# RWKV's chunk inverse: corrections of X and its transpose on 32 of 64 columns

## The chip, the cores and the metric

One of the eight cores of a Trainium2 chip runs the whole program. The metric is the device time of one execution in microseconds. The kernel before took 3782.82 us, the median of 3 runs (3780.62 to 3784.01).

## The reference, cut to what matters

The program computes two transformer-like blocks on 512 tokens of width 1024. The first block has four branches; the change sits in the fourth, RWKV-7, with 16 heads of 64. Its recurrence over the tokens is

```python
def step(state, inp):
    r_t, w_t, k_t, v_t, kk_t, b_t = inp
    sk = jnp.einsum('bhvk,bhk->bhv', state, kk_t)
    state = (state * w_t[:, :, None, :] - sk[..., None] * b_t[:, :, None, :]
             + v_t[..., None] * k_t[:, :, None, :])
    return state, jnp.einsum('bhvk,bhk->bhv', state, r_t)
```

The kernel does this in 8 chunks of 64 tokens. Inside a chunk the dependence of each token on the ones before it is a triangular system, so each chunk and head needs the inverse of a unit triangular 64x64 matrix.

## The kernel before, in words

`rwkv_core_phase` (line 1137 on) is one phase among many. Its first TensorE work stands at about 1237 us of the trace and its last at about 1560 us; projections with 512-column matmuls come before and after. It handles the heads in 8 pairs. A pair's 8 chunks of 2 heads are 16 matrices of 64x64, laid out in one plane of 128 partitions by 512 columns: partitions 0 to 63 hold one matrix of a cell, partitions 64 to 127 another, and the 512 columns are 8 cells of 64 (`cell(h, i)`).

The inverse is built by levels. X and its transpose XT start as the inverse of the 2x2 diagonal blocks (`step_lt`, lines 1591 to 1599). Level n, for n from 1 to 5, joins neighbouring blocks of 2^n columns in three steps:

- Y{n}: TensorE forms Y from LM and X, where LM is the system's matrix under the mask of the level. GpSimd makes LM (line 1503, `level_mask`); ScalarE copies Y out of PSUM (line 1443).
- X{n}: TensorE forms the correction from XT and Y, and VectorE subtracts it from X (line 1575).
- XT{n}: TensorE forms the correction of the transpose from Y and XT, and VectorE subtracts it from XT (line 1575). At level 5 only the transpose is needed: Y5 is a product by `cells` (line 1246), and XT5 as well, subtracted at line 1583.

Each of these steps is 16 fp32 matmuls, one for each 64x64 matrix, each with its own weights (64x64) and 64 moving columns. `blocks64` (line 1254) and `cells` (line 1246) issue them alternating between the two diagonal quarters of the array. The trace shows each fp32 matmul as two records of weight load and two of matmul, so a step is 32 records of each. `products` (line 1239) uses all four quarters of the array in turn.

The order of the work is written out by hand. Time goes in blocks `b` of 16 beats. In block b, pair b is prepared (VectorE lines 1605 to 1614, GpSimd 1503, ScalarE 1484 to 1489); pair b-1 goes through list `A` (X0, then Y, X, XT of levels 1 to 4); pair b-2 goes through list `B` (level 5, the transposes of v, kappa, k and beta by `turn`, the masked products Lk, Ak, Ab with their evictions at line 1589, LkV, NU0, WT); pair b-3 goes through its 8 chunks of state recurrence (PE 1354, 1361, 1371, 1378, 1381; VectorE 1624, 1634); pair b-4 is finished (normalisation, lines 1640 to 1660). Each engine takes its part of each beat strictly in program order, and semaphores tie the engines together. Block 1 has only list A and preparation; blocks 3 to 7 have all of it; from block 9 on list A is empty.

Two orders matter below. At beat 2 and 3 VectorE has, in this order: the subtraction for XT5, a state step (1634), three preparations of pair b (1608, 1609, 1611), the subtraction for X1 and the masked eviction of Lk (1589). And TensorE's `turn` of k at beat 4 (`trkt`, line 1261) writes the PSUM bank that Lk is read from, so it waits for that eviction, with everything behind it.

Of the kernel before, what the change touches and what calls it, by code (L numbers as in the profile page):

```python
# [13 lines left out]
ALU = mybir.AluOpType  # L14
# [6 lines left out]
T = 512  # L21
TT = T // P
# [1114 lines left out]
def rwkv_core_phase(k, r, kk, v, sg, a, norm, hs, w, last=()):  # L1137
# [5 lines left out]
    nc = k.nc  # L1143
# [3 lines left out]
    LT, LM, X, XT, Y = (lambda p, n=n: own(5 * (p % 2) + n) for n in range(5))  # L1147
# [7 lines left out]
    cell = lambda h, i: slice(256 * h + 64 * i, 256 * h + 64 * i + 64)  # L1155
    half = lambda q: slice(64 * q, 64 * q + 64)
    chunk = lambda i, q: slice(P * i + 64 * q, P * i + 64 * q + 64)
    by_head = lambda h, i: slice(P * i + 64 * h, P * i + 64 * h + 64)
    quad = lambda ap: ap.rearrange("p (h i c) -> p h i c", h=2, i=TT)
    eight = lambda ap: ap.rearrange("p (n c) -> p n c", c=64)  # L1160
    two_banks = lambda b: k.ps[:, b:b + 2, 0:256].rearrange("p h (i c) -> p h i c", i=TT)
    mask = lambda ap: ap.unsqueeze(1).unsqueeze(1).broadcast_to([P, 2, TT, 64])
    mask8 = lambda ap: ap.unsqueeze(1).broadcast_to([P, 8, 64])
# [10 lines left out]
    A = ["X0"] + [f"{s}{n}" for n in (1, 2, 3, 4) for s in ("Y", "X", "XT")]  # L1174
# [5 lines left out]
    a_made, a_act, a_dve = k.sem("w_a_made"), k.sem("w_a_act"), k.sem("w_a_dve")  # L1180
# [35 lines left out]
    def users_before(s):  # L1216

        n = B.index(s)
        found = [[t for t in range(n) if b in B_BANKS[t]] for b in B_BANKS[n]]
        return [B[f[-1]] if f else None for f in found]  # L1220
# [5 lines left out]
    with nc.Block() as block:  # L1226
# [7 lines left out]
        def _(pe):  # L1234
# [7 lines left out]
            def cells(l, r, b, r_cell=cell):  # L1242
                for h in range(2):
                    for i in range(TT):
                        for q in range(2):
                            ins = nc.tensor.matmul(k.bank(b)[half(q), cell(h, i)], l[half(q), cell(h, i)], r[half(q), r_cell(h, i)], start=True, stop=True)
                return ins

            def blocks64(l, r, b):
                for h in range(2):  # L1250
                    for i in range(TT):
                        for q in range(2):
                            other = k.const("ident")[half(q), half(q)] if r is None else r[half(q), cell(h, i)]
                            ins = nc.tensor.matmul(k.bank(b)[half(q), cell(h, i)], l[half(q), cell(h, i)], other, start=True, stop=True)  # L1254
                return ins

            def turn(src, b, by):
                for i in range(TT):
                    t = slice(i * P, (i + 1) * P)
                    if by is None:  # L1260
                        ins = nc.tensor.transpose(k.bank(b)[:, t], src[:, t], k.const("ident"))
                    else:
                        ins = nc.tensor.matmul(k.bank(b)[:, t], src[:, t], by, start=True, stop=True)
                return ins

            def step_a(p, s):
                b = A.index(s) % 2
                if s == "X0":
                    pe.wait_ge(lt_out, p + 1)
                    if p >= 1:  # L1270
                        pe.wait_ge(*a_out(p - 1, "XT4"))
                    ins = blocks64(XT(p), None, b)
                elif s[0] == "Y":
                    n = int(s[1:])
                    pe.wait_ge(lm_ok, 4 * p + n)
                    pe.wait_ge(*a_out(p, f"X{n - 1}"))
                    ins = blocks64(LM(p), X(p), b)
                elif s[:2] == "XT":
                    pe.wait_ge(*a_out(p, "Y" + s[2:]))
                    ins = blocks64(Y(p), XT(p), b)  # L1280
                else:
                    pe.wait_ge(*a_out(p, "Y" + s[1:]))
                    if s != "X1":
                        pe.wait_ge(*a_out(p, f"XT{int(s[1]) - 1}"))
                    ins = blocks64(XT(p), Y(p), b)
                ins.then_inc(a_made, 1)

            def step_b(p, s):
                b = B_BANKS[B.index(s)][0]
                for user in users_before(s):  # L1290
                    if user is not None:
                        pe.wait_ge(*b_out(p, user))
                    else:
                        pe.wait_ge(lt_read, min(p + 2, PAIRS))
                        if p >= 1:
                            pe.wait_ge(*b_out(p - 1, "Ab"))
                if s == "Y5":
                    pe.wait_ge(lm5_ok, p + 1)
                    pe.wait_ge(*a_out(p, "X4"))
                    ins = cells(LM(p), X(p), b)  # L1300
                elif s == "XT5":
                    pe.wait_ge(*b_out(p, "Y5"))
                    ins = cells(Y(p), XT(p), b)
                elif s == "trv":
                    ins = turn(pl(v + p), b, None)
                elif s == "trkap":
                    ins = turn(pl(sg + p), b, None)
                elif s == "trkt":
                    pe.wait_ge(pool_ok, 6 * p + 6)
                    ins = turn(pl(kk + p), b, None)  # L1310
                elif s == "trbt":
                    ins = turn(pl(a + p), b, None)
                elif s == "Lk":
                    pe.wait_ge(pool_ok, 6 * p + 6)
                    ins = products(pl(kk + p), pl(sg + p), b)
                elif s == "Ak":
                    ins = products(pl(kk + p), pl(r + p), b)
                elif s == "Ab":
                    ins = products(pl(a + p), pl(r + p), b)
                elif s == "LkV":  # L1320
                    pe.wait_ge(*b_out(p, "Lk"))
                    pe.wait_ge(*b_out(p, "trv"))
                    ins = cells(LKK, VT(p), b, by_head)
                elif s == "NU0":
                    pe.wait_ge(*b_out(p, "LkV"))
                    pe.wait_ge(*b_out(p, "XT5"))
                    ins = cells(XT(p), LKV, b)
                elif s == "WT":
                    pe.wait_ge(*b_out(p, "trkap"))
                    for i in range(TT):  # L1330
                        for q, h in ((0, 0), (1, 1), (0, 1), (1, 0)):
                            ins = nc.tensor.matmul(k.bank(b + q)[half(h), 64 * i:64 * i + 64], KAPT[half(q), by_head(h, i)], XT(p)[half(q), cell(h, i)],
                                                   start=True, stop=True)
                ins.then_inc(b_made, 1)
# [51 lines left out]
            for b in range(BLOCKS):  # L1386
                for beat in range(16):
                    if 3 <= b < PAIRS + 3:
                        p, j = b - 3, beat // 2
# [33 lines left out]
                    for m in range(*gate_steps(b, beat)):  # L1423
                        n, q = divmod(m, KT)
                        if n < len(last):
                            if q == 0:
# [3 lines left out]
                                if n >= 4:  # L1430
                                    pe.wait_ge(gate_out, n - 3)
                            ins = nc.tensor.matmul(k.bank(n % 4), slot(n)[:, q * P:(q + 1) * P], last[n][1](q), start=(q == 0), stop=(q == KT - 1),
                                                   skip_group_check=True)
# [127 lines left out]
        def _(dve):  # L1561
            link = lambda ins: k.dve_chain(dve, ins)

            def step_a(p, s):
                if not on_dve(s):
                    return
                dve.wait_ge(a_made, a_made_at(p, s))
                x = XT(p) if s[1] == "T" else X(p)
                if s == "X1":
                    dve.wait_ge(*a_out(p, "X0"))  # L1570
                elif s == "XT1":
                    dve.wait_ge(lt_out, p + 1)
                else:
                    dve.wait_ge(*a_out(p, s[:-1] + str(int(s[-1]) - 1)))
                nc.vector.tensor_tensor(x, x, k.bank(A.index(s) % 2), ALU.subtract).then_inc(a_dve, 1)

            def step_b(p, s):
                if not on_dve(s):
                    return
                dve.wait_ge(b_made, b_made_at(p, s))  # L1580
                if s == "XT5":
                    dve.wait_ge(*a_out(p, "XT4"))
                    ins = nc.vector.tensor_tensor(XT(p), XT(p), k.bank(2), ALU.subtract)
                elif s == "WT":
                    out = WR(p).rearrange("p (i b c) -> p i b c", i=TT, b=4)[:, :, 0::3, :].rearrange("p i q c -> p q i c")
                    ins = nc.vector.tensor_tensor(out, two_banks(2), before(p).rearrange("p i q -> p q i").unsqueeze(3).broadcast_to([P, 2, TT, 64]), ALU.mult)
                else:
                    dst, m = {"Lk": (LKK, strict), "Ak": (AK(p), incl), "Ab": (AB(p), incl)}[s]
                    ins = nc.vector.tensor_tensor(quad(dst), two_banks(2), mask(m), ALU.mult)
                ins.then_inc(b_dve, 1)  # L1590
# [1475 lines left out]
```

## Time and profile before

| what | value |
|---|---|
| time, median of 3 runs | 3782.82 us |
| the profiled execution's own time | 3787.06 us |
| its span in the trace | 3785.3 us |
| mean granted TensorE clock | 0.951 of full speed |
| PE busy | 3411.5 us (90%) |
| DVE busy | 1218.5 us (32%) |
| ACT busy | 580.8 us (15%) |
| POOL busy | 684.1 us (18%) |

PE is TensorE's matmul side and PEld its weight loads; DVE is VectorE, ACT ScalarE, POOL GpSimd. Busy time is a union: overlapping records count once, and a record's time includes the latency until its result is written. PEclk is the granted TensorE clock as a share of 2.4 GHz; it has two levels, 1.00 (2.4 GHz) and 0.50 (1.2 GHz), and a mean between them says how long each held.

### The profile page before, as it was taken

Reading aid. Unit: us, or ns where it says so; the run is one execution under the profiler, and the core shown is the slowest. Engines: PE = TensorE matmul, PEld = TensorE weight load, DVE = VectorE, ACT = ScalarE, POOL = GpSimd, SP = SyncE. Lnnn points to the kernel's source line nnn. Section 1 sums busy time; section 2 is a strip of 40 time slices with the busy share of each in tenths; the row PEclk is TensorE's granted clock in tenths of the full one; section 3 lists DMA queues with packets and bytes.
Section 4 is the critical chain, followed back from the end, with each engine's and each line's share of the span. In section 5 each row is a group of like instructions: output and inputs, shape, how many; then the busy total and the mean of one; then the engine's idle time right before and its main releaser. Section 6 shows DMA issues by size and latency. Waiting matters only on the chain. (4 is left out here: it accounts for less than half of the span.)

```text
span 3785.3 us, 43454 instructions
## 1 busy us (share of the span) xinstructions
PE 3411.5 (90%) x18392; PEld 1842.3 (49%) x18392; DVE 1218.5 (32%) x2054; ACT 580.8 (15%) x1070; POOL 684.1 (18%) x432
## 2 busy tenths in 40 slices
PE   8989999999999898989999999998687885889887
PEld 3454444743443787434444445476676743322222
DVE  1443051023122566203442045316556533001112
ACT  1033030001002233101000011115232301100001
POOL 0000010000000553005995500006322200000000
PEclk9999999998999899999999989999898997999999
DMA  4211223210320000323353322223000011599996
GB/s 155 70 37 45 73 72 101 78 45 28 106 78 23 3 3 22 111 66 112 122 155 124 117 60 68 67 62 90 1 1 1 1 46 72 200 409 409 409 409 244
DMA packets 120512, 406.19 MB, mean 107 GB/s; under 512 B 13825, under 2 KB 18561, under 8 KB 120065
## 3 DMA queue, kind: packets, MB, share of 16 engines
q1 hardware_dynamic: 113408, 378.25, 28.2%
q0 software_dynamic: 6912, 25.17, 2.1%
q8 instruction: 147, 2.41, 0.3%
q14 instruction: 45, 0.36, 0.0%
HBM read 399.17 MB, written 4.19 MB: 107 GB/s over the span
## 5 line engine op out<-in xcount | busy, mean ns | idle before, releaser
L422 PE MATMUL ps<-arena 128*128 128x512 f32 (+1 forms) x3936 | 1684.7, 590 | 63.8 <-DVE arena L565 17.2
L422 PEld LDWEIGHTS ps<-arena 128*128 128x128 f32 x3936 | 754.3, 193 | 991.9 <-issue 967.5
L2640 PE MATMUL ps<-arena 128*64 128x512 f32 x1024 | 244.9, 601 | 32.3 <-DMA arena<-in_w_gate 15.7
L1503 POOL TENSOR_TENSOR arena<-arena 128x512 f32<-128x512 f32 x64 | 80.2, 1270 | 752.0 <-DVE arena L1605 658.7
L2235 PE MATMUL ps<-arena 128*128 128x128 f32 x1312 | 174.7, 295 | 23.5 <-POOL arena L2290 21.1
L473 DVE SCALAR_TENSOR_TENSOR arena<-ps,params,arena 128x511 f32<-128x511 f32 (+4 forms) x266 | 190.7, 717 | 9.5
L2744 POOL TENSOR_SCALAR arena<-arena,small 128x1024 f32<-128x1024 f32 x64 | 183.5, 2867 | 8.1 <-DMA arena<-in_w_mod 4.1
L2235 PEld LDWEIGHTS ps<-arena 128*128 128x128 f32 x1312 | 167.6, 206 | 28.5 <-issue 14.9
L467 DVE TENSOR_SCALAR arena<-ps,params 128x512 f32<-128x512 f32 x68 | 55.1, 810 | 377.3 <-PE ps L422 377.3
L2640 PEld LDWEIGHTS ps<-arena 128*64 128x64 f32 x1024 | 70.9, 136 | 200.5 <-issue 197.5
L2706 DVE SCALAR_TENSOR_TENSOR arena<-ps,mods,arena 128x512 f32<-128x512 f32 x64 | 48.1, 751 | 371.9 <-PE ps L2628 371.1
L416 PE MATMUL ps<-arena 128*128 128x128 f32 (+1 forms) x1120 | 143.8, 289 | 10.2 <-DVE arena L568 10.2
L1870 POOL TENSOR_SCALAR arena<-arena,small 128x768 f32<-128x768 f32 x32 | 70.2, 2206 | 444.1 <-DVE small L1850 444.1
L416 PEld LDWEIGHTS ps<-arena 128*128 128x128 f32 x1120 | 142.8, 212 | 14.1 <-issue 9.3
L453 ACT ACTIVATE arena<-arena 128x512 f32<-128x512 f32 (+2 forms) x60 | 36.1, 601 | 693.2 <-DVEq L477 693.2
L2668 PE MATMUL ps<-arena 128*64 128x512 f32 x512 | 120.5, 612 | 23.8 <-DMA arena<-in_w_down 14.4
L444 ACT ACTIVATE arena<-ps 128x512 f32<-128x512 f32 (+1 forms) x75 | 43.1, 575 | 618.1 <-PE ps L422 524.9
L2746 POOL TENSOR_TENSOR arena<-arena 128x1024 f32<-128x1024 f32 x56 | 132.1, 2358 | 4.7
L304 PE MATMUL ps<-arena 128*128 128x512 f32 x256 | 117.7, 612 | 6.1 <-ACT arena L313 4.2
L1254 PE MATMUL ps<-arena 64*64 64x64 f32 x3072 | 115.0, 226 | 3.1 <-ACT arena L1443 2.5
L1254 PEld LDWEIGHTS ps<-arena 64*64 64x64 f32 x3072 | 104.8, 139 | 11.0 <-issue 7.1
L2275 ACT ACTIVATE arena<-ps 128x512 f32<-128x512 f32 x132 | 78.9, 597 | 180.9 <-PE ps L2235 124.2
(407 smaller groups left out, 3231.5 us busy)
## 6 DMA issues: line engine op xcount, KB each, us to landing
arena<-in_w_in SPq DMA_DIRECT2D x166, 512.0 KB, 3.6
arena<-in_w_gate SPq DMA_DIRECT2D x128, 512.0 KB, 15.5
arena<-in_w_up SPq DMA_DIRECT2D x128, 512.0 KB, 15.5
arena<-in_w_down SPq DMA_DIRECT2D x128, 512.0 KB, 15.6
arena<-in_w_mod POOLq DMA_DIRECT2D x48, 512.0 KB, 4.2
arena<-in_ffn_up SPq DMA_DIRECT2D x44, 512.0 KB, 3.6
arena<-in_w_branch SPq DMA_DIRECT2D x32, 512.0 KB, 3.6
arena<-in_w_out SPq DMA_DIRECT2D x16, 512.0 KB, 3.6
```

What stands on the lines that cost most here:

```text
L304: ins = k.nc.tensor.matmul(k.bank(self.banks[i % len(self.banks)]), w[:, q * P:(q + 1) * P], self.fills[i][1](q), start=(q == 0), stop=(q ...
L416: last = nc.tensor.matmul(out[:, t * m:(t + 1) * m], j["rhs"](ka + q)[:, t * P:(t + 1) * P], w[:, q * m:(q + 1) * m], start=(q == 0), stop ...
L422: last = nc.tensor.matmul(out[0:m, 0:j["n"]], w[:, q * m:(q + 1) * m], j["rhs"](ka + q), start=(ka + q == 0), stop=(ka + q == kt - 1))
L473: ins = nc.vector.scalar_tensor_tensor(out=o, in0=s, scalar=c, in1=o, op0=ALU.mult, op1=ALU.add)
L1254: ins = nc.tensor.matmul(k.bank(b)[half(q), cell(h, i)], l[half(q), cell(h, i)], other, start=True, stop=True)
L1503: tt = lambda o, x, y, op: nc.gpsimd.tensor_tensor(o, x, y, op)
L2235: mm = lambda l, r: nc.tensor.matmul(out, l, r, start=True, stop=True)
L2275: nc.scalar.activation(dst, k.bank(n % BANKS), ACT.Copy).then_inc(act_out, 1)
L2640: ins = nc.tensor.matmul(k.bank(b + f)[64 * e:64 * e + 64, :], xev(q, 2 * p + e), slot(g + e)[:, f * 512:f * 512 + 512], start=(q == 0), s ...
L2668: ins = nc.tensor.matmul(k.bank(6 + f)[64 * e:64 * e + 64, :], HT(u)[:, q * P + 64 * e:q * P + 64 * e + 64], slot(g + e)[:, f * 512:f * 51 ...
L2744: k.pool_chain(pool, nc.gpsimd.tensor_scalar(o, w(m), c, None, ALU.mult))
L2746: k.pool_chain(pool, nc.gpsimd.tensor_tensor(a, a, o, ALU.add))
```

## The change

In X{n} and XT{n} of levels 1 to 4 and in XT5, a matmul now streams only the 32 of 64 columns that the level changes: of each pair of neighbouring groups of 2^n columns the first (`odd` 0) for X, the second (`odd` 1) for XT. It writes them to the same places in PSUM. The subtraction on VectorE runs over the same 256 of 512 columns in place of all 512. Weights, number of instructions, banks, semaphores and order stay; so do X0, the Y steps, and all other products. The columns come in runs of 2, 4, 8, 16 and 32 elements at levels 1 to 5, with gaps of the same length.

```diff
+    side_of = lambda ap, n, odd: ap.rearrange("p (m z c) -> p m z c", z=2, c=1 << n)[:, :, odd, :]
+    sides_of = lambda ap, n, odd: ap.rearrange("p (e m z c) -> p e m z c", e=8, z=2, c=1 << n)[:, :, :, odd, :]
...
+            def blocks32(l, r, b, n, odd):
+                for h in range(2):
+                    for i in range(TT):
+                        for q in range(2):
+                            ins = nc.tensor.matmul(side_of(k.bank(b)[half(q), cell(h, i)], n, odd), l[half(q), cell(h, i)],
+                                                   side_of(r[half(q), cell(h, i)], n, odd), start=True, stop=True)
+                return ins
...
                     pe.wait_ge(*a_out(p, "Y" + s[2:]))
-                    ins = blocks64(Y(p), XT(p), b)
+                    ins = blocks32(Y(p), XT(p), b, int(s[2:]), 1)
...
-                    ins = blocks64(XT(p), Y(p), b)
+                    ins = blocks32(XT(p), Y(p), b, int(s[1:]), 0)
...
                     pe.wait_ge(*b_out(p, "Y5"))
-                    ins = cells(Y(p), XT(p), b)
+                    ins = blocks32(Y(p), XT(p), b, 5, 1)
...
-                nc.vector.tensor_tensor(x, x, k.bank(A.index(s) % 2), ALU.subtract).then_inc(a_dve, 1)
+                n, odd = int(s[-1]), int(s[1] == "T")
+                x = sides_of(x, n, odd)
+                nc.vector.tensor_tensor(x, x, sides_of(k.bank(A.index(s) % 2), n, odd), ALU.subtract).then_inc(a_dve, 1)
...
-                    ins = nc.vector.tensor_tensor(XT(p), XT(p), k.bank(2), ALU.subtract)
+                    x = sides_of(XT(p), 5, 1)
+                    ins = nc.vector.tensor_tensor(x, x, sides_of(k.bank(2), 5, 1), ALU.subtract)
```

## Rows read from the trace of the kernel before

**Rows 1.** Page: busy shares; by stretch: length, PE PEld DVE ACT POOL, PEclk, DMA, GB/s.

```profile
PE 3411.5 (90%) x18392; PEld 1842.3 (49%) x18392; DVE 1218.5 (32%) x2054; ACT 580.8 (15%) x1070; POOL 684.1 (18%) x432
...
1240.00:1540.00 300.00, 270.48 (x6919) 229.31 (x6920) 181.88 (x385) 90.12 (x155) 131.83 (x111) 0.96 0.04 12
```

**Rows 2.** Instruction groups by form: busy, mean ns of one | idle before, releaser.

```profile
L1254 PE MATMUL ps<-arena 64*64 64x64 f32 x3072 | 115.0, 226 | 3.1 <-ACT arena L1443 2.5 <-issue 0.6
L1246 PE MATMUL ps<-arena 64*64 64x64 f32 x1024 | 39.9, 224 | 0.2
L1575 DVE TENSOR_TENSOR arena<-arena,ps 128x512 f32<-128x512 f32 x64 | 43.7, 685 | 35.9 <-PE ps L1254 35.5
L1583 DVE TENSOR_TENSOR arena<-arena,ps 128x512 f32<-128x512 f32 x8 | 5.5, 687 | 19.8 <-PE ps L1246 19.8
L2157 DVE TENSOR_TENSOR arena<-ps,arena 128x256 f32<-128x256 f32 x4 | 1.7, 425 | 27.7 <-PE ps L2081 27.7
L1586 DVE TENSOR_TENSOR arena<-ps,small 128x512 f32<-128x512 f32 x8 | 5.5, 685 | 0.7 <-PE ps L1332 0.7
```

**Rows 3.** Waits of PE from 1240 to 1500 us: total, times, longest.

```profile
PE ps L1261 <- DVE arena L1589: 14.2, 8, 2.4
PE ps L1261 <- ACT arena L1466: 3.3, 6, 0.5
PE ps L1254 <- ACT arena L1443: 2.5, 5, 0.7
...
PE ps L1354 <- DVE arena L1634: 1.2, 5, 0.3
```

**Rows 4.** Timeline, steady state: start, length, engine, line, count [idle before].

```profile
1383.35 1.07 PEld L1254 LDWEIGHTS ps<-arena 64*64 64x64 f32 x32
...
1384.28 0.60 PEld L1239 LDWEIGHTS ps<-arena 64*64 64x64 f32 x32
```

**Rows 5.** Narrow and wide streams, line 416 alone, by stretch (16 columns, then 128).

```profile
189.00:192.36 3.36, 3.36 (x33) 3.36 (x32) 1.00 0.27 107
192.36:194.40 2.04, 2.04 (x12) 2.04 (x12) 0.50 0.00 0
697.50:700.90 3.40, 3.40 (x33) 3.40 (x32) 1.00 0.23 93
```

**Rows 6.** Durations by line, minimum/median/maximum in ns.

```profile
L1254 PEld LDWEIGHTS ps<-arena x3072: 129/135/223, 1244.1 to 1490.1; 64*64 64x64 f32 x192
L416 PEld LDWEIGHTS ps<-arena x1120: 186/192/338, 186.6 to 3168.6; 128*128 128x128 f32 x187
L416 PE MATMUL ps<-arena x1120: 179/275/582, 187.1 to 3168.6; 128*128 128x128 f32 x149, 128*128 128x16 f32 x38
```

**Rows 7.** Timeline, VectorE's queue ahead of TensorE's longest stall, block 7.

```profile
1433.21 0.69 DVE L1583 TENSOR_TENSOR arena<-arena,ps 128x512 f32<-128x512 f32 x1 [2.49 <-PE ps L1246]
1433.82 0.58 DVE L1634 SCALAR_TENSOR_TENSOR arena<-arena,small,ps 64x64 f32<-64x64 f32 x2
...
1436.28 0.68 DVE L1575 TENSOR_TENSOR arena<-arena,ps 128x512 f32<-128x512 f32 x1
...
1436.88 0.68 DVE L1589 TENSOR_TENSOR arena<-ps,cst 128x512 f32<-128x512 f32 x1
...
1437.62 0.65 PE L1261 MATMUL ps<-cst,arena 128*128 128x128 f32 x4 [2.30 <-DVE arena L1589]
```

**Rows 8.** Block 1 by stretch; columns as in rows 1, PEclk third from last.

```profile
1243.67:1247.09 3.42, 2.72 (x39) 2.09 (x40) 1.90 (x3) 1.51 (x3) 0.91 (x1) 0.50 0.02 5
1247.09:1250.50 3.41, 3.41 (x70) 3.41 (x68) 0.69 (x1) 0.00 (x0) 3.41 (x4) 0.50 0.01 2
1250.50:1253.91 3.41, 2.71 (x92) 2.57 (x89) 2.25 (x3) 0.60 (x1) 3.41 (x4) 1.00 0.02 5
```

**Rows 9.** Timeline of block 1: one step at 1.2 GHz, three at 2.4.

```profile
1244.11 1.78 PEld L1254 LDWEIGHTS ps<-arena 64*64 64x64 f32 x32 [1.50 <-issue]
...
1252.16 3.04 PEld L1254 LDWEIGHTS ps<-arena 64*64 64x64 f32 x96 [0.84 <-ACT arena L1443]
```

## Prediction, on record before the result was known

> **What bounds the kernel now.** I read the page's busy shares first, then the busy time by stretch, then the groups by form and the waits of the stretch that the change touches. TensorE is busy for 90% of the span, and between 1240 and 1540 us, where the chunk inverse runs, for 270 of 300 us, while VectorE has 182 there [rows 1]. So in this phase TensorE is nearly the bound, and a gain comes in only two ways: TensorE's own stream gets shorter, or a wait that it sits in gets shorter. The waits of TensorE in the phase are few: 14.2 us in 8 waits of line 1261 for VectorE's line 1589, 3.3 and 2.5 us for ScalarE, 1.2 us for the state step 1634 [rows 3]. None of them names line 1575, the subtraction that gets cheaper. That subtraction rather waits for TensorE, 35.5 us in all, and 1583 waits 19.8 us [rows 2].
>
> **How many instructions change.** X1 to X4, XT1 to XT4 and XT5 are 9 steps for each of 8 pairs, 72 steps. Each is 32 records on TensorE, 2304 of the 4352 that lines 1254 and 1246 hold (3072 and 1024 from the arena [rows 2], and 256 of X0, by its identity), and one subtraction on VectorE, 64 of line 1575 and 8 of line 1583.
>
> **TensorE's stream: no gain.** A step of 32 records issues its loads over 1.07 us, one load's own 0.13 us included, so 0.94 us over 31 gaps, 30 ns a record [rows 4]. It alternates between two quarters of the array, so one quarter takes a record every 60 ns. The products of line 1239, on four quarters, need 0.60 us for the same number: 15 ns a record, again 60 ns a quarter [rows 4]. 64 columns of fp32 would stream in about this time, so this alone doesn't tell whether the stream or the weight load sets the pace. Line 416 does: with 16 moving columns it passes 33 records in 3.36 us, with 128 moving columns 33 in 3.40 us, both against weights of 128 columns and both at full clock [rows 5]. The stream's width makes no difference there: the load of the weights paces it, at 3.4/32 = 106 ns or a little more for 128 columns. How the load scales with its columns is in the shortest durations: 186 ns for 128 columns, 129 ns for 64 [rows 6], so 57 ns for 64 columns more. Loads of 64 columns then want some 57 ns a quarter, and the pace is 60 now. With 32 moving columns each quarter still loads 64 columns of weights twice a matmul, and the pace stays 57 to 60. I take 0. The bounds: were the stream alone the pace, 2304 records would fall from 30 to 15 ns, a gain of 34.6 us. In the other direction the strided reads (runs of 2 to 32 elements, which no row shows on TensorE) may cost more than a dense column; up to twice as much hides under the load, beyond that each step would lengthen. At four times, 72 steps would double and lose 68 us. The nearest row is line 416, whose pace ignored the stream, so 0.
>
> What does get shorter is a step's last record: 275 ns is the median with mostly 128 columns [rows 6] and 226 the mean with 64 [rows 2], about 50 ns for 64 columns, so some 25 ns for the 32 that go. It counts only where someone waits for the step.
>
> The Trainium skill, page "TensorE: Matmul & The Clock Gate", section "Back-to-back issue gap", gives the gap of a lone stream as its columns over 2.4 GHz plus 2.5 ns; by that formula the change would halve the pace, which is the rival of the full gain below. Rows 5 deny it for streams that load weights each time.
>
> **VectorE: 0.26 us off each of 72 subtractions.** 512 columns take 685 ns, 256 take 425 ns in line 2157, a tensor_tensor from PSUM as well [rows 2]. That is 0.26 us less, 18.7 us of VectorE's busy time. Line 1586 writes pieces of 64 with gaps at the dense pace of 685 ns [rows 2]; runs of 2 are not in the trace. At worst a strided element costs double and the gain is 0; I take the full 0.26. Most of this is idle time of VectorE, which costs nothing. It pays in two places.
>
> First, the longest stall. Line 1261 (the turn of k) waits for the eviction of Lk at 1589, and VectorE comes to that through a queue that starts with XT5's subtraction: 1583 at 1433.21, then 1634, 1608, 1609, 1611, 1575 at 1436.28, 1589 at 1436.88, and TensorE goes on at 1437.62 after 2.30 us idle [rows 7]. VectorE has no idle time in that queue once 1583 starts, so whatever gets shorter in it comes off the stall in full: 0.26 (1583) + 0.26 (1575) + 0.025 (XT5's last record is done sooner) = 0.55 us. It happens in blocks 2 to 8, and in block 9 without 1575: 7 x 0.55 + 0.29 = 4.1 us of the 14.2. After it the same wait is still the last one, being 1.8 us long where it was 2.3.
>
> Second, the wait of 1354 for the state step 1634, 5 times and 1.2 us in all [rows 3], where a 1575 stands just ahead in VectorE's queue: it goes, 1.2 us. What is late next there is TensorE's own order. Sum of the gains: 5.3 us.
>
> **The clock, where the change costs.** While line 416 streamed 16 columns, TensorE and its loads were busy for every bit of the stretch, and yet the granted clock was 1.00 in 189.0 to 192.4 us and 0.50 right after, from 192.4 to 194.4. With 128 columns, equally busy, it was 1.00 [rows 5]. So keeping the engine occupied with loads doesn't hold the 2.4 GHz level; streamed columns do. The change thins the streamed columns of two steps in three to half, at the same pace. Where the engine is at full clock that is probably still enough, since the thin steps stand among full ones. But the phase starts at 1.2 GHz: 0.50 up to 1250.5, and 1.00 from there, after a stretch (1247.09 to 1250.50) filled without a gap by X1 and XT1, which had 64 columns each [rows 8]. Those two are now thin, and block 1 has nothing but list A to follow. I expect the clock not to rise at 1250.5 but only in block 2, where Y5, X0, the turns and the masked products stream in full. The price: a step takes 1.78 us of loads at 1.2 GHz and 3.04/3 = 1.01 at 2.4 [rows 9], so 0.76 more. Left in block 1 after 1250.5 are Y2 to XT4, 9 steps: 6.9 us. Add two more steps before the rise in block 2, 1.5 us: 8.4 us. That row of 416 decides for me; the cost lies between 0 (the clock rises as before) and, if it stays low through block 2 as well, about twice that, 17 us.
>
> The same page of the Trainium skill, "Part 1: The HAM clock gate", says that activity releases the throttle and advises to keep TensorE busy without gaps. Read as the engine being occupied, that rule would give the clock back at 1250.5 as before, since X1 and XT1 leave no gap, and the sum would be the gain alone; rows 5 speak against this reading.
>
> **The sum.** -4.1 - 1.2 + 8.4 = +3.1 us on the profiled execution's 3787.06 us. That execution is 4.24 us above the median of the runs shown, 3782.82, so I move the median by the same amount: 3785.9, told as 3786. Later phases have no changed instruction; they only move against the instants at which the clock changes. 0.2%, 7.6 us, is about what a measurement of this kernel can tell from no change.
>
> **The rivals.**
> - *The clock rises as before.* Only the gain is left: 3782.8 - 5.3 = 3777.5. For it: the engine is as busy as before, and rows 5 have 16 columns, much thinner than half. Chance 0.28.
> - *The stream halves too.* 34.6 us from TensorE and 5.3 from the waits: 3743. For it: 64 columns of fp32 fit the 60 ns pace just as well. Against it: rows 5 and 6. Part of it is possible, if small loads are cheaper than I read them. Chance 0.08.
> - *Slower: the thin stream lowers the clock again and again.* One mechanism: in each full block (3 to 8) the 2.3 us stall [rows 3, 7] comes beside thin steps, and the clock falls where it held before. It decides the sign as soon as three more falls come on top of the late rise. Each costs some 2 us (2 to 3 steps at 0.76 more), 5 to 6 of them 11 us: 3786 + 10 = 3796. Against it: the shorter stall. Chance 0.13.
> - *The change saves nothing on VectorE*, because runs of 2 to 8 elements cost as much as the gaps between them. No gain, and the clock's cost in part: 3783 to 3791. Chance 0.08.
> - The forecast as above, own range 3780 to 3791. Chance 0.43.
>
> **How the numbers follow.** Faster by over 0.2% (below 3775.2): all of the second rival and a quarter of the first, 0.15. Slower by over 0.2% (above 3790.4): most of the third, a tenth of the forecast and a little of the fourth, 0.20. Within: 0.65. The range leaves out the full halving and the far half of the repeated falls, and takes in the rest: 3772 to 3797.
>
> **What would show each step.** A changed step's 32 loads still take 1.0 to 1.07 us at full clock; at 0.55 the stream was the pace and I am wrong. The subtractions show 425 ns for 128x256 at every level. The wait of 1261 for 1589 is about 10 us in place of 14.2. The granted clock between 1250.5 and 1262 us is 0.50, with about 1.78 us a step, and X0 to XT4 of block 1 end near 1268 and not at 1262. If it is 1.00 there, the first rival holds. If the mean clock of 1265 to 1500 falls clearly, the third does.

## The result, and the profile after

The changed kernel took 3795.44 us, the median of 6 runs (3793.55 to 3800.38), against 3781.83 (3777.86 to 3784.01, 6 runs) before: a ratio of 1.0039, 95% interval 1.0026 to 1.0052. It is slower by 13.6 us, where 3.1 us and a time of 3786 were forecast. The time lies inside the stated range of 3772 to 3797, near its upper end, and in the case that had a chance of 0.20. The two profiled executions, which the traces below come from, differ by 9.6 us.

The page's busy shares and the stretch of the inverse, to be read against [rows 1]: the page's line on the engines, then the stretch from the trace (length, busy time of PE, PEld, DVE, ACT and POOL, granted clock, DMA share, GB/s):

```profile
PE 3426.8 (90%) x18392; PEld 1854.9 (49%) x18392; DVE 1206.2 (32%) x2054; ACT 580.9 (15%) x1070; POOL 682.8 (18%) x432
```

```profile
1240.00:1540.00 300.00, 275.78 (x6844) 238.31 (x6843) 164.16 (x376) 88.77 (x152) 128.04 (x109) 0.90 0.04 12
```

VectorE lost busy time, as it should. TensorE gained some, at the same number of instructions, and its granted clock in the stretch is 0.90 where it was 0.96. The groups and durations of the changed steps, against [rows 2, 6] (name, busy and mean as there):

```profile
L1263 PE MATMUL ps<-arena 64*64 64x32 f32 x2304 | 90.5, 231 | 3.0 <-ACT arena L1453 2.3 <-issue 0.7
L1587 DVE TENSOR_TENSOR arena<-arena,ps 128x256 f32<-128x256 f32 x64 | 26.8, 420 | 45.2 <-PE ps L1263 45.1
```

The weight loads of the changed line alone (minimum/median/maximum, then the stretch):

```profile
L1263 PEld LDWEIGHTS ps<-arena x2304: 129/135/228, 1244.2 to 1504.1; 64*64 64x64 f32 x192
```

And one changed step at full clock, against [rows 4]: 32 loads still take about a microsecond.

```profile
1398.51 1.01 PEld L1263 LDWEIGHTS ps<-arena 64*64 64x64 f32 x32 [0.76 <-issue]
```

The longest wait of TensorE, against [rows 3] (1271 was 1261, 1602 was 1589):

```profile
PE ps L1271 <- DVE arena L1602: 10.9, 8, 1.9
```

So the work is what the change says: half the columns on both engines. The stall, that is TensorE's wait in line 1271 for the eviction of Lk, is 3.3 us shorter in sum. The time shows up when the phase is cut at each X0, the start of a pair's list A. First blocks 1, 2, 3 and 5 before (length, busy time of the five engines, granted clock, DMA), then blocks 1, 2, 3 and 6 after:

```profile
1240.20:1263.60 23.40, 21.00 (x487) 18.39 (x489) 11.92 (x17) 5.36 (x9) 14.72 (x12) 0.78 0.01 3
1263.60:1289.60 26.00, 23.23 (x734) 21.05 (x731) 13.58 (x22) 8.51 (x15) 13.93 (x12) 1.00 0.01 3
1289.60:1322.80 33.20, 28.43 (x864) 25.37 (x862) 20.16 (x43) 9.82 (x17) 14.16 (x13) 1.00 0.01 3
...
1357.60:1391.30 33.70, 30.60 (x874) 26.80 (x872) 24.84 (x51) 12.76 (x21) 18.31 (x16) 1.00 0.01 3
```

```profile
1237.60:1268.80 31.20, 29.05 (x486) 26.44 (x488) 9.63 (x18) 5.36 (x9) 15.77 (x13) 0.50 0.01 2
1268.80:1298.40 29.60, 27.30 (x733) 24.67 (x731) 11.90 (x21) 8.72 (x15) 12.87 (x12) 0.83 0.01 3
1298.40:1333.70 35.30, 31.44 (x865) 28.12 (x862) 18.64 (x43) 9.90 (x17) 15.17 (x13) 0.90 0.01 3
...
1403.50:1436.60 33.10, 30.43 (x879) 26.86 (x874) 23.13 (x50) 12.66 (x21) 18.38 (x16) 1.00 0.02 4
```

Block 1 is 7.8 us longer and runs at 0.50 throughout; block 2 is 3.6 us longer at 0.83 in place of 1.00. Among the full blocks, one at clock 1.00 is even a little shorter than before (33.1 us, block 6, against 33.7, block 5 before). One in which the clock fell is longer: block 3 takes 35.3 us at 0.90, where before it took 33.2 at 1.00.

### The profile page after: what moved, and what is told of

Its sections match the earlier page's. It is cut to its first block and busy times, and to the rows that moved or that the text cites. A ratio compares the mean times of both kernels' runs of the same rounds, so it can differ in the third digit from the quotient of the medians.

```text
span 3794.9 us, 43454 instructions
## 1 busy us (share of the span) xinstructions
PE 3426.8 (90%) x18392; PEld 1854.9 (49%) x18392; DVE 1206.2 (32%) x2054; ACT 580.9 (15%) x1070; POOL 682.8 (18%) x432
## 5 line engine op out<-in xcount | busy, mean ns | idle before, releaser
L2653 PE MATMUL ps<-arena 128*64 128x512 f32 x1024 | 246.3, 605 | 31.5 <-DMA arena<-in_w_gate 14.3
L416 PE MATMUL ps<-arena 128*128 128x128 f32 (+1 forms) x1120 | 143.8, 288 | 10.2 <-DVE arena L568 10.2
L2681 PE MATMUL ps<-arena 128*64 128x512 f32 x512 | 120.1, 611 | 23.1 <-DMA arena<-in_w_down 13.7
L1263 PE MATMUL ps<-arena 64*64 64x32 f32 x2304 | 90.5, 231 | 3.0 <-ACT arena L1453 2.3
L2303 POOL TENSOR_TENSOR arena<-arena,cst 128x512 f32<-128x512 f32 x60 | 67.5, 1145 | 122.7 <-PE ps L2248 64.8
```

The source lines that it names most:

```text
L416: last = nc.tensor.matmul(out[:, t * m:(t + 1) * m], j["rhs"](ka + q)[:, t * P:(t + 1) * P], w[:, q * m:(q + 1) * m], start=(q == 0), stop ...
L1263: ins = nc.tensor.matmul(side_of(k.bank(b)[half(q), cell(h, i)], n, odd), l[half(q), cell(h, i)], side_of(r[half(q), cell(h, i)], n, odd), ...
L2653: ins = nc.tensor.matmul(k.bank(b + f)[64 * e:64 * e + 64, :], xev(q, 2 * p + e), slot(g + e)[:, f * 512:f * 512 + 512], start=(q == 0), s ...
L2681: ins = nc.tensor.matmul(k.bank(6 + f)[64 * e:64 * e + 64, :], HT(u)[:, q * P + 64 * e:q * P + 64 * e + 64], slot(g + e)[:, f * 512:f * 51 ...
```

## The experiments

Twelve experiments ran; e11 is the kernel before itself and e12 is e1 once more. "Phase" is the time from the first spread of the norm (line 1402 before, at 1226 us, some 11 us ahead of the first products) to the last gate product (1432) in the run's one profile. It is given to within 0.3 us, the same way in every row. "Half clock" is how much of it the trace's record of the granted clock has at 1.2 GHz. The ratio is to the kernel before, run beside it on the same chip, with its 95% interval; that kernel's median was 3781.9 to 3782.5 us there.

| kernel | phase, us | half clock, us | median, us | ratio to before |
|---|---|---|---|---|
| before | 335.1 | 34.1 | 3781.83 | |
| the change | 346.1 | 75.1 | 3795.44 | 1.0039 (1.0026 to 1.0052) |
| e1, subtractions alone | 329.8 | 34.1 | 3783.62 | 1.0003 (0.9993 to 1.0012) |
| e2, matmuls alone | 356.5 | 88.7 | 3803.53 | 1.0056 (1.0043 to 1.0069) |
| e3, thin in pair 0 | 338.1 | 54.6 | 3792.06 | 1.0026 (1.0017 to 1.0035) |
| e4, thin in pairs 1 to 7 | 335.8 | 51.2 | 3786.25 | 1.0011 (1.0002 to 1.0020) |
| e5, 32 weight columns too | 325.0 | 41.0 | 3775.77 | 0.9984 (0.9975 to 0.9993) |
| e6, 16 moving columns | 353.2 | 95.6 | 3805.61 | 1.0060 (1.0044 to 1.0075) |
| e7, the change, waits filled | 340.2 | 34.1 | 3789.83 | 1.0020 (1.0011 to 1.0028) |
| e8, e1, waits filled | 337.8 | 27.3 | 3785.20 | 1.0007 (0.9998 to 1.0015) |
| e9, e1 reordered | 328.6 | 27.3 | 3778.71 | 0.9991 (0.9982 to 1.0000) |
| e10, the change reordered | 334.8 | 51.2 | 3783.47 | 1.0002 (0.9993 to 1.0012) |
| e11, before again | 332.0 | 27.3 | 3785.10 | 1.0005 (0.9997 to 1.0014) |
| e12, e1 again | 334.5 | 44.4 | 3783.89 | 1.0001 (0.9992 to 1.0010) |

**e1, only the subtractions.**

```diff
-                    ins = blocks32(XT(p), Y(p), b, int(s[1:]), 0)
+                    ins = blocks64(XT(p), Y(p), b)
```

and likewise for XT and, with `cells`, XT5.

> Only VectorE's half is kept: all matmuls stream 64 columns again, the subtractions run over 256 of 512 columns. My theory (TensorE's pace is the weight load's; the loss is the 2.4 GHz level that thin streams fail to earn or hold; VectorE's part is a gain): the clock is back at 2.4 GHz at about 1250 us as before, the wait of the turn of k for Lk's eviction stays near 11 us where it was 14.2, and the kernel is 4 to 6 us faster than before, 3776 to 3778. Rival (the strided access on VectorE or something that it lets start earlier costs the time): no faster than before, or slower by as much as the change, 3782 to 3795.

The profile did what the theory said: the clock is up in block 1 as before (0.78), the phase is 5.3 us shorter at equal time at 1.2 GHz, the stall is 11.5 us. The median did not: it is 3783.62, a ratio of 1.0003, where 3776 to 3778 was expected, and it lies in the span of the rival. That VectorE's part costs the 13.6 us is out, since e1 is level with before; but the gain is not in the times either. That led to e11 and e12.

**e2, only the matmuls** (32 moving columns; the subtractions run over all 512 columns, so the columns that a level leaves alone are spoilt).

> Only TensorE's half is kept: 32 moving columns, but the subtractions run over all 512 columns again, so the columns that the level doesn't change are corrupted by what the bank held. My theory: the clock stays at 1.2 GHz to about 1270 us and falls more often later, as with the change, and the longest stall is back at 14 us: 4 to 6 us slower than the change, 3799 to 3802. Rival (the loss sits on VectorE): 3777 to 3784.

It is the slowest but one, with the stall back at 14.4 us. It stands 8.1 us above the change by the medians and 6.4 by the ratios, somewhat more than expected. So the loss is TensorE's half, and VectorE's half does gain, here where it is taken away.

**e3 and e4, where it is lost.** The thin matmuls under a condition on the pair, the short subtractions everywhere:

```diff
-                    ins = blocks32(XT(p), Y(p), b, int(s[1:]), 0)
+                    ins = blocks32(XT(p), Y(p), b, int(s[1:]), 0) if p == 0 else blocks64(XT(p), Y(p), b)
```

with `p >= 1` in e4.

> 32 moving columns for pair 0 alone, 64 for pairs 1 to 7; subtractions over 256 columns for all. My theory: block 1 stays at 1.2 GHz past 1250 us and costs 8 to 12 us against the kernel with 64 columns throughout (e1), the later blocks hold their clock as there: 3785 to 3789. Rival (the loss comes from further falls of the clock in the full blocks, not from the late rise): equal to e1, 3776 to 3778.

> The reverse: 64 moving columns for pair 0, 32 for pairs 1 to 7; subtractions over 256 columns for all. My theory: the clock rises at about 1250 us as before; the full blocks see two or three more stretches at 1.2 GHz, 3 to 7 us: 3780 to 3785. Rival (the loss comes from the full blocks): 3790 to 3796. If e3 and e4 exceed e1 by amounts that add up to what the change exceeds e1 by, the two places are independent.

e3 is 0.0023 above e1 in ratio, 8.7 us, e4 0.0008, 3 us; the change is 0.0036, 13.6 us, above e1, and 11.7 is their sum. Both medians came near what was expected (e3 3792.06, 3 us above 3789; e4 3786.25, 1 us above 3785). The intervals of e3 and e1 are apart. Those of e4 and e1 overlap, so the part of the full blocks is not clear of noise in the times. In the profiles e3's phase is 8.3 us longer than e1's, e4's 6.0 and the change's 16.3. So the late rise is the larger part of the loss, between a half and three quarters, and the full blocks are the rest. Blocks 1 and 2, first of e1, then of e3:

```profile
1239.30:1262.20 22.90, 20.56 (x486) 18.11 (x488) 9.25 (x17) 5.36 (x9) 14.72 (x12) 0.78 0.01 3
1262.20:1287.40 25.20, 22.84 (x738) 20.80 (x733) 12.53 (x22) 8.50 (x15) 13.92 (x12) 1.00 0.01 3
```

```profile
1239.50:1270.70 31.20, 29.07 (x486) 26.46 (x488) 9.60 (x17) 5.36 (x9) 15.79 (x13) 0.50 0.01 2
1270.70:1299.10 28.40, 25.94 (x734) 23.58 (x733) 11.96 (x21) 8.70 (x15) 12.87 (x12) 0.89 0.01 3
```

Thin steps in the first pair alone cost 8.3 us in block 1 and 3.2 in block 2. The clock does not rise in block 1; it does so 3 us into block 2 and falls once more there for 3.4 us. The later blocks have two short falls where e1 has four, which is why the whole phase is only 8.3 us longer.

**e5 and e6, what sets the pace.** e5 loads 32 of the 64 weight columns (half of each correction's rows are left out); e6 streams 16 columns, half of those that change, so both leave out part of the result. The edit of e5:

```diff
+                            w32 = slice(256 * h + 64 * i, 256 * h + 64 * i + 32)
...
-                                                   l[half(q), cell(h, i)],
+                                                   l[half(q), w32],
```

> As the change, but the matmuls of the X and XT steps load only the first 32 of 64 weight columns, so half of the rows of each correction are left out. It tells whether the load sets the pace. My theory (the load paces): records of a step come every 15 to 18 ns in place of 28 to 30, a step's loads take about 0.6 us in place of 1.0, and the streamed columns fill as much of the time as 64 columns did, so the clock holds better than with the change. Switching the array's tile size for each step may add up to 0.2 us a step. 3765 to 3790. Rival (issue or streaming paces, not the load): the pace stays at 28 to 30 ns.

> As the change, but with 16 moving columns, half of those that the level changes; the others are left as they are in the bank. My theory: the pace at full clock stays at 28 to 29 ns a record, and the clock falls more still: 90 to 200 us of the phase at 1.2 GHz (75 with the change), 3800 to 3840. Rival (the stream's length sets the pace, or the clock goes by occupation and not by streamed columns): records closer together, or a clock as with the change, 3785 to 3797.

One step of each at full clock, e5 first:

```profile
1388.93 0.58 PEld L1264 LDWEIGHTS ps<-arena 64*32 64x32 f32 x32
```

```profile
1400.49 1.01 PEld L1264 LDWEIGHTS ps<-arena 64*64 64x64 f32 x32 [0.76 <-issue]
```

With half the weight columns a step's loads take 0.58 us. With 16 moving columns and full weights they take 1.01, as with 32 and with 64 [rows 9]. The load paces these matmuls; moving columns below 64 neither cost nor save here. e5 has the same thin stream as the change, but packed closer, and only 41.0 us at 1.2 GHz to the change's 75.1. Its clock rises after 20.5 us, as before, and block 1 has 0.76 with TensorE occupied for 17.73 of 21.50 us. The change has 0.50 there with 29.05 of 31.20 us occupied. e6 has a thinner stream at the same pace and 95.6 us. So in these runs the time at 1.2 GHz does not go with how much of the time TensorE is occupied; it went up as the stream got thinner and down as it was packed closer.

**e7 and e8, filling the waits.** Twenty 512-column matmuls on constants into bank 5, which the first pairs don't use, 14 before the first `step_lt`, 3 before X0 and 3 before Y1 of pair 0:

```diff
+            def fill(count):
+                for _ in range(count):
+                    nc.tensor.matmul(k.bank(5), k.const("ident"), k.const("chunkstart"), start=True, stop=True)
```

> The change, with 20 matmuls of 512 columns on constants put into a bank that is not yet in use, in TensorE's waits before the first pair's products (14), its X0 (3) and its Y1 (3). My theory: the clock holds 2.4 GHz from about 1225 us on, through block 1 if thin steps can hold it; about 8 us of the loss come back: 3783 to 3789. Rival (thin steps beside the waits of block 1 let it fall anyway): 3792 to 3797.

> 64 moving columns, subtractions over 256 (e1), with the same 20 matmuls in the waits. My theory: the 20.5 us at 1.2 GHz at the phase's start go, of which some 10 held work; the phase gets 3 to 6 us shorter than in e1 (329.8 us) and the kernel is at 3774 to 3780, below both kernels. Rival (the filling delays the real products as much as it gives): the same as e1, 3780 to 3785.

Blocks 1 and 2 of e7, with thin steps:

```profile
1241.90:1264.30 22.40, 19.34 (x493) 15.87 (x494) 9.20 (x17) 5.25 (x9) 14.36 (x12) 1.00 0.01 3
1264.30:1291.20 26.90, 24.58 (x738) 22.26 (x733) 12.45 (x22) 8.53 (x15) 13.90 (x12) 0.94 0.02 4
```

Block 1 takes 22.4 us where the change takes 31.2, at the full clock throughout, thin or not. Here thin steps held the level that they had not brought back in the change. e7's median is 5.6 us below the change's and 0.8 above the expected span. After block 1 its clock falls eight times, 34.1 us in all, about as in the change.

e8 missed: 3785.20, where 3774 to 3780 was expected, and a phase 8.0 us longer than e1's. X0 of pair 0 starts 2.3 us later after the phase's start (16.6 against 14.3 us), and e1 had little work to speed up in its 20.5 us at 1.2 GHz, since TensorE was idle for 9.9 of them. Block 1 came out 0.5 us shorter. The rest is a fall in block 2 (1.8 us) and one of 10.2 us at 1507 us (4.4 us from the last X0 to the end). e6 and e10 have a fall there too, of the same length, and e1 has not; that the filling caused it is not shown.

**e9 and e10, the stall ahead of the falls.** On VectorE the three preparations of beat 3 go behind the eviction of Lk:

```diff
-                    if b < PAIRS:
+                    if b < PAIRS and beat != 3:
                         prepare(b, beat)
...
                             step_b(b - 2, s)
+                    if b < PAIRS and beat == 3:
+                        prepare(b, beat)
```

> e1 (64 moving columns, subtractions over 256), and on VectorE the three preparations of beat 3 (2.0 us) stand behind the eviction of Lk in place of ahead of it. My theory: the wait of the turn of k for that eviction, 11.5 us in 8 waits in e1, falls to 1 to 2 us; the falls of the clock in blocks 3 to 7, which follow that stall, go with it. The phase is 10 to 16 us shorter than e1's 329.8 and the kernel at 3767 to 3775. Rival (what waits next takes the place: the preparations come late for GpSimd or the next pair's products): 3778 to 3784.

> The change with the same reordering. My theory: the stall goes here too, but thin steps still miss the clock's rise in block 1, so it stays 10 to 16 us above e9: 3780 to 3788. Rival (the stall alone made the clock fall, thin or not): within 5 us of e9.

```profile
PE ps L1364 <- DVE arena L1647: 5.2, 6, 1.0
PE ps L1256 <- POOL arena L1513: 3.4, 2, 3.0
PE ps L1271 <- DVE arena L1602: 3.2, 7, 0.8
```

```profile
1255.13 1.97 PE L1256 MATMUL ps<-arena 64*64 64x64 f32 x32 [3.02 <-POOL arena L1513]
```

The first fence holds waits of TensorE in e9, the second one line of its timeline. The stall of 1271 is 3.2 us in place of 11.5, and no fall of the clock is left in blocks 2 to 8. Blocks 2 to 7 are 7.2 us shorter than e1's. But TensorE waits 5.2 us for the state step 1647 now. In block 1 the late preparations reach GpSimd late, TensorE waits 3.0 us for its mask of level 3, and the clock falls there once: the block takes 28.9 us against 22.9. So the phase is only 1.2 us shorter than e1's, where 10 to 16 was expected, and the rival has the number: 3778.71 in its 3778 to 3784. e9 is still the fastest kernel that computes everything, its interval just touching 1.

e10 is level with before and 4.8 us above e9. The first is in the theory's span (3780 to 3788), the second in the rival's (within 5 us); the 10 to 16 us between the two were not there, because e9 lost time of its own in block 1. Blocks 1 and 2 of e10:

```profile
1239.80:1269.80 30.00, 27.20 (x486) 24.64 (x488) 10.29 (x17) 5.36 (x9) 14.74 (x12) 0.54 0.01 2
1269.80:1294.50 24.70, 23.17 (x733) 21.02 (x731) 12.39 (x22) 8.49 (x15) 13.87 (x12) 1.00 0.02 3
```

Against the change, e10 is the test of the full blocks. Its steps are as thin, its stall is 3.6 us in place of 10.9, and in blocks 2 to 8 the clock falls once for 3.4 us, where the change has five falls and 30.7 us. Its median is 12.0 us below the change's. Where neither has a fall, e9 and e10 take the same time (31.4 and 31.4 us in block 3, 32.6 and 32.6 in block 4), so thin steps neither cost nor save anything there. The timelines say the same. With 64 columns and the original order (before, e1, e8, e11, e12) there are 19 falls in blocks 2 to 8, and each stands beside a wait of line 1261 or 1271 for Lk of 1.2 to 2.4 us. Of the change's five, three stand beside such a wait of 1.9 us and two beside waits of 1.1 and 0.9 us only.

**e11 and e12, the scatter.**

> The kernel before itself, for a second profile of it on the chip on which e12 runs. Theory and rival alike: ratio 1.000 within its interval. Its phase tells how much one execution's falls of the clock move: I expect 334 to 338 us, with 3 or 4 falls after 1260 us.

> e1 again. In e1's profile the phase was 5.25 us shorter than in the profile before at equal time at 1.2 GHz, but the median of its runs did not move. If the gain is real and lost in the scatter of the clock over the whole program, the profile repeats 328 to 332 us and the ratio comes out at 0.9985 to 0.9995. Rival (VectorE's gain is not there): phase 334 us and more, ratio 1.000 or above.

e11's phase came out a little shorter than expected, with two falls. e12's phase is in the rival's span, as is its ratio of 1.0001. Two profiles of one kernel differ by 3.1 us of phase at 6.8 us of half clock (before, e11) and by 4.7 at 10.3 (e1, e12): 0.45 us for each microsecond at 1.2 GHz, both times. Taking that off, 0.45 times the half clock, leaves 319.7 for before and e11, 314.5 for e1 and e12, 316.6 for e2, 313.5 and 312.8 for e3 and e4, and 312.3 for the change. So the short subtractions are worth 5.2 us of the phase at an equal clock; before and e1 show it without the factor, at 34.1 us each. The 2 to 3 us that this leaves for the thin matmuls are not shown. They hang on a factor that was read from differences of 7 and 10 us and is put on 41 here: e3 against e1 gives 0.40 (8.3 us for 20.5), and with that nothing is left, as in e9 and e10.

Why the medians show none of the 5.2 us stays open. e1 and e12 have four and five falls in their full blocks, the two profiles of before three and two, which would give back some of it; but e1's four last no longer than the three of before (13.7 us each). And outside the phase, where no instruction changed, the time moves from 3447.3 to 3454.0 us between these four profiles.

## Why the prediction came out as it did

The forecast was a loss of 3.1 us and the measured one is 13.6, more than four times as much. That the range holds the time is owed to the third rival, which it took in.

- **TensorE's pace, 0 expected: right.** 1.01 us a step after, and e5 and e6 show it is the load. One reading was low: records of line 416 start 112 ns apart, with 16 moving columns and with 128; the 33 of [rows 5] include those that reach over the stretch's ends.
- **VectorE, 0.26 us off each subtraction: right.** 420 ns against 685 at runs of 2 to 32 elements. The stall fell by 3.3 us (4.1 expected), the wait for the state step went, and 5.2 us at equal clock stand against the 5.3 of the sum. But no median shows this gain: e1 and e12 are level with before.
- **The late rise, 8.4 us: right in kind, a little small.** Block 1 ran at 0.50 to its end, 31.2 us with 1.75 us for each thin step, as [rows 8, 9] scaled. It cost 8.3 us there (e3 against e1), and the clock rose 3 us into block 2. Blocks 1 and 2 together cost 11.5 us, of which some 1.5 are the fall in block 2 (3.4 us at 0.45), an estimate, so that 10.0 are the late rise. That the engine was occupied did not help. In the change it had no gap at all over 13.5 us around the end of block 1, at 1.2 GHz throughout:

```profile
1258.20:1271.70 13.50, 13.50 (x235) 12.64 (x232) 4.80 (x8) 2.90 (x5) 3.45 (x3) 0.50 0.01 2
```

- **The step that failed** is this one: "Where the engine is at full clock that is probably still enough, since the thin steps stand among full ones." It was enough in block 1 of e7, and in the full blocks of e10, where the stall is gone. Beside the stall it was not: after 1278 us the change has five stretches at 1.2 GHz, 30.7 us in all, where before has three, 13.7 us. At 0.45 that is 7.7 us, a term that the sum had at nothing. Forecast and third rival came true together, and the sum needed both: 10.0 + 7.7, less the gain of 5.2, is 12.5, and the phase grew by 11.0 between the two profiles. I had priced that rival at 10 us on top of the forecast and given it 0.13, arguing that the shorter stall speaks against it. It did not prevent it: with waits of 1.9 us where they were 2.4 the clock fell more often, in e1 and e12 as well.
- By the Trainium skill, "TensorE: Matmul & The Clock Gate", "Part 1: The HAM clock gate", activity releases the throttle. Read as being occupied, the runs deny it: the change had TensorE occupied for 29.05 of block 1's 31.20 us and stayed at 1.2 GHz, while before had it occupied for 21.00 of 23.40 us and got 0.78.

What stays open: what exactly the chip counts, and where the 5.2 us of VectorE's half go. Each kernel but before and e1 has a single profile, and where the falls land differs between two profiles of one kernel, so the counts of falls are no better than that. And e9 with the preparations moved only from block 2 on, which would leave block 1 alone, was not tried.

## What to carry to other kernels

For a stream of fp32 matmuls that each load their own weights, see first which of the two sets the pace. Here it was the load: with 64 weight columns, 64, 32 and 16 moving columns all took 1.01 us a step, and 32 of each took 0.58 (e5). So cutting moving columns saved nothing on TensorE, and it cost clock: 34.1, 75.1 and 95.6 us of the phase at 1.2 GHz. Before thinning a stream, look for the places where the clock has to come back after a wait, and for waits that return in every block; taking such a wait away (e10 against the change, 12.0 us) was worth nearly all of the loss. And where a phase's clock falls come from a regular stall, judge a gain of a few microseconds by medians of several executions and by time at equal clock, not by one profile.

## What the runs showed of the hardware that I had not expected

In these runs holding the clock and getting it back were different. Thin steps held 2.4 GHz for all of block 1 once it was there (e7, 1.00 over 22.4 us), and did not bring it back in 31.2 us of the same steps (the change, 0.50; e3 as well). It is not a strict line: in e10, also thin, it came back at 1267.1 us, 2.7 us before block 1 ended, after Y4 and a set of products, which stream 64 columns. And records of matmuls can follow each other fast: 32 loads of 32 columns on two quarters of the array took 0.58 us (e5), 0.10 of it one load's own length, so 15 ns each.
